# Key norms around the start of attention: an earlier scaling, a root by Newton steps, and work moved between attention's first blocks

## The chip, the cores and the metric

One core of a Trainium2 chip. The metric is the device time of one execution in microseconds; three executions of the kernel before gave 1094.52, 1094.96 and 1095.26 us, median 1094.96.

## The reference, cut to what matters

One decoder block of 512 tokens, width 1024. The part around the change is the attention with eight heads: queries and keys are normalised by head, rotated and scored in 128-query blocks.

```python
kv = (rms_norm(kv_lat, g_kva) @ w_kvb).reshape(B, S, H, QK_NOPE + V_DIM)
k_nope = rms_norm(kv[..., :QK_NOPE], g_k_nope)
v = kv[..., QK_NOPE:]
...
def block(args):
    q_i, i = args
    s = jnp.einsum('bhqd,bhkd->bhqk', q_i, kh).astype(jnp.float32)
    ...
    prob = jax.nn.softmax(s, axis=-1).astype(vh.dtype)
    return jnp.einsum('bhqk,bhkd->bhqd', prob, vh)
```

`rms_norm` multiplies by the reciprocal root of the mean square. For the keys this is one number for each token and head.

## The kernel before, in words

Each engine runs a queue of its own, written out by hand; semaphores order them. The stage ahead of attention takes eight steps `s`: steps 0 to 3 project two query heads each, steps 4 to 7 two key heads with their values. In a step TensorE multiplies four token tiles in three passes (high and low parts of fp32), ScalarE writes each tile out of PSUM with its squares and takes a root, and VectorE sums the squares (128 rows x 8 numbers: four tiles by two heads), forms the mean (`mean`, L1409), takes ScalarE's root back as a reciprocal and scales the keys with it (L1774; for the last step `last_k_norm`, L1779 to L1782). `link` makes VectorE wait for an instruction of its own before the next one reads its result. Then TensorE transposes the two heads (`head_T`, by L2141), which waits for the semaphore `qk_n`, and for the PSUM bank, which VectorE frees as it evacuates the heads before (`k_evac`, L1743). `rope_low` (L1730) makes the low parts of one head's rotated query rows, in two halves.

Attention has 32 blocks (8 heads by 4 query blocks; within a head in the order 1, 4, 2, 3 key tiles wide, the last head 1, 2, 3, 4). In the loop's pass `s` TensorE makes the scores of block `s` (L2328 to L2333), transposes the probabilities of block `s` - 1 (L2343) and multiplies those of block `s` - 2 with the values (L2352). The first block of a head waits for that head's rope rows (semaphore `rope_lo`). VectorE takes the maximum of block `s` (L1805), then the reciprocal sum and the scaling of block `s` - 2 (L1811, L1814). ScalarE takes the exponential (L1163) and copies the transposed probabilities. GpSimd adds each scaled block to the other branch (L795) and, between two such additions, splits the output weights: a high part (L804) after even blocks, a low part (L807) after odd ones.

The last two key heads are used from block 24 on. Their transposes stand in TensorE's loop at `s` = 5. SyncE's loads for the stage after attention wait until all 32 blocks are added.

Of the kernel before, what the change touches and what calls it, by code (L numbers as in the profile page):

```python
# [6 lines left out]
def hybrid_block_kernel(nc, a, out):  # L7
# [24 lines left out]
    I32, U32 = mybir.dt.int32, mybir.dt.uint32  # L32
# [45 lines left out]
    with ctx:  # L78
# [827 lines left out]
        def _(act):  # L906
# [194 lines left out]
            for s in range(9):  # L1101
                if s == 6:
                    rope_high(0)
                    rope_high(1)
                if s < 8:
                    for t in range(NT):
                        n = P_Q + 4 * s + t
                        act.wait_ge(pj_done, n + 1)
                        if t == 0:
                            if s >= 1:  # L1110
                                act.wait_ge(qk_ms, s)
                            if 2 <= s < 6:
                                act.wait_ge(tr_done, T_Q + 3 * (s - 2) + 2)
                                act.wait_ge(q_rot, s - 1)
                            elif s >= 6:
                                act.wait_ge(tr_done, step_T(s - 2))
                            if s == 0:
                                act.wait_ge(ln_v, NT)
                        b_ = bank[n % 4]
                        if s < 4:  # L1120
                            src = b_[:, 0:2 * QK].rearrange("p (h d) -> p h d", h=2)
                            act.activation(qc[s % 2][:, t], src, ACT.Copy)
                            act.activation(sqc[:, t], src, ACT.Square).then_inc(pj_free[n % 4], 1)
                        else:
                            src = b_[:, :].rearrange("p (h d) -> p h d", h=2)
                            c = s - 4
                            act.activation(qc[s % 2][:, t, :, 0:NOPE], src[:, :, 0:NOPE], ACT.Copy)
                            act.activation(sqc[:, t, :, 0:NOPE], src[:, :, 0:NOPE], ACT.Square)
                            act.activation(V[:, t, 2 * c:2 * c + 2, :], src[:, :, NOPE:], ACT.Copy).then_inc(pj_free[n % 4], 1)
                        if t == (0 if s == 6 else 1) and s + 1 < 8:  # L1130
                            qkv_split(s + 1)
                if s == 7:
                    T = T_K + 4
                    act.wait_ge(tr_done, T + 1)
                    act.activation(kT[:, 4, :], bank[4 + T % 2][:, :], ACT.Copy).then_inc(tr_free[T % 2], 1)
                if 1 <= s <= 4:
                    c = s - 1
                    for h in range(2):
                        T = T_Q + 3 * c + h
                        act.wait_ge(tr_done, T + 1)  # L1140
                        act.activation(qT[:, 2 * c + h, :], bank[4 + T % 2][:, :], ACT.Copy, scale=gqk).then_inc(tr_free[T % 2], 1)
                if s < 8:
                    act.wait_ge(qk_ms, s + 1)
                    n = 16 if s < 4 else 8
                    act.activation(ssq[:, 0:n], msq[:, 0:n], ACT.Sqrt).then_inc(qk_rt, 1)
# [254 lines left out]
        def _(dve):  # L1400
            steps = [0]

            def link(ins):
                steps[0] += 1
                ins.then_inc(dve_step, 1)
                dve.wait_ge(dve_step, steps[0])
# [318 lines left out]
            def rope_low(h, halves=(0, 1)):  # L1725
                r0, r1 = ROPE * (h % 2), ROPE * (1 - h % 2)
                dve.wait_ge(rope_hi, h + 1)
                for half in halves:
                    cols = slice(half * SEQ // 2, (half + 1) * SEQ // 2)
                    dve.tensor_tensor(q_st[r1:r1 + ROPE, h % 2, cols], qrT[r0:r0 + ROPE, h // 2, cols],  # L1730
                                      q_st[r0:r0 + ROPE, h % 2, cols].bitcast(F32), ALU.subtract).then_inc(rope_lo, 1)
# [2 lines left out]
                gate_a(g)  # L1734

            def k_evac(c, b0):
                if c == 1:
                    rope_low(0)
                    rope_low(1)
                for h in range(1 if c == 2 else 0, 2):  # L1740
                    T = T_K + 2 * c + h
                    dve.wait_ge(tr_done, T + 1)
                    dve.tensor_copy(kT[:, 2 * c + h, :], bank[b0 + T % 2][:, :]).then_inc(tr_free[T % 2], 1)  # L1743

            for s in range(8):
                if 2 <= s <= 5:
                    T = T_Q + 3 * (s - 2) + 2
                    dve.wait_ge(tr_done, T + 1)
                    dve.tensor_copy(qrT[:, s - 2, :], bank[4 + T % 2][:, :]).then_inc(tr_free[T % 2], 1)
                if s + 1 < 8:  # L1750
                    qkv_split(s + 1)
                if s < 8:
                    sq = sqc.rearrange("p t h d -> p (t h) d")
                    if s == 7:
                        dve.wait_ge(pj_free[1], (P_Q + 4 * s) // 4 + 1)
                        link(dve.tensor_reduce(ssq[:, 0:4], sq[:, 0:4, 0:NOPE], AX.X, ALU.add))
                    dve.wait_ge(pj_free[3], (P_Q + 4 * s) // 4 + 1)
                    if s < 4:
                        link(dve.tensor_reduce(ssq[:, 8:16], sq[:, :, NOPE:QK], AX.X, ALU.add))
                    r0 = 4 if s == 7 else 0  # L1760
                    link(dve.tensor_reduce(ssq[:, r0:8], sq[:, r0:8, 0:NOPE], AX.X, ALU.add))
                    if s < 4:
                        mean(msq[:, 8:16], ssq[:, 8:16], ROPE, EPS)
                    mean(msq[:, 0:8], ssq[:, 0:8], NOPE, EPS).then_inc(qk_ms, 1)
                if 5 <= s < 7:
                    k_evac(s - 5, 4)
                if s < 7:
                    dve.wait_ge(qk_rt, s + 1)
                    n = 16 if s < 4 else 8
                    link(dve.reciprocal(msq[:, 0:n], ssq[:, 0:n]))  # L1770
                    z = qc[s % 2].rearrange("p t h d -> p (t h) d")
                    if s < 4:
                        dve.tensor_tensor(z[:, :, NOPE:QK], z[:, :, NOPE:QK], rep(msq[:, 8:16], [P, 8, ROPE], 2), ALU.mult)
                    dve.tensor_tensor(z[:, :, 0:NOPE], z[:, :, 0:NOPE], rep(msq[:, 0:8], [P, 8, NOPE], 2),  # L1774
                                      ALU.mult).then_inc(qk_n, 1)

            def last_k_norm():
                dve.wait_ge(qk_rt, 8)
                link(dve.reciprocal(msq[:, 0:8], ssq[:, 0:8]))  # L1779
                z = qc[1].rearrange("p t h d -> p (t h) d")  # L1780
                dve.tensor_tensor(z[:, :, 0:NOPE], z[:, :, 0:NOPE], rep(msq[:, 0:8], [P, 8, NOPE], 2),
                                  ALU.mult).then_inc(qk_n, 1)  # L1782
# [10 lines left out]
            for s in range(NA + 2):  # L1793
                if s == NA + 1:
                    mT_low(0)
                if s == 1:
                    k_evac(2, 4)
                if s == 2:
                    last_k_norm()
                if s == 7:  # L1800
                    k_evac(3, 6)
                if s < NA:
                    W = (head_block(s)[1] + 1) * P
                    dve.wait_ge(s_done, s + 1)
                    dve.tensor_reduce(nm[:, s % 4:s % 4 + 1], bank[s % 2][:, 0:W], AX.X, ALU.max,  # L1805
                                      negate=True).then_inc(nm_ready, 1)
                if s >= 2:
                    n = s - 2
                    h, i = head_block(n)
                    dve.wait_ge(pv_done, n + 1)  # L1810
                    link(dve.reciprocal(rinv[:, n % 4:n % 4 + 1], rs[:, n % 4:n % 4 + 1]))  # L1811
                    if n >= 2:
                        dve.wait_ge(ya_add, n - 1)
                    dve.scalar_tensor_tensor(otmp[n % 2], bank[2 + n % 2][:, 0:VD], rinv[:, n % 4:n % 4 + 1],  # L1814
                                             sigb[:, i, h * VD:(h + 1) * VD], ALU.mult, ALU.mult).then_inc(o_ready, 1)
                if s % NT < 2 and 2 <= s // NT + 1 < H:
                    rope_low(s // NT + 1, (s % NT,))
# [317 lines left out]
        def _(pe):  # L2135
# [176 lines left out]
            for i in range(4):  # L2312
                pe.wait_ge(pj_free[i], P_WO // 4)
            for s in range(NA + 2):
                if s == 5:
                    head_T(7, b0=6)
                if s == 2 * H:
                    for i in range(2):
# [323 lines left out]
```

## Time and profile before

| | |
|---|---|
| median of three executions | 1094.96 us |
| the profiled execution, its own time | 1094.87 us |
| its span in the profile | 1093.1 us |
| TensorE's, VectorE's, ScalarE's, GpSimd's busy share | 98%, 85%, 74%, 38% |
| TensorE's granted clock, in all 40 slices | 9 (90% of full speed or more) |
| the eight projection steps end at | about 272 us |
| attention | about 273 to 337 us |

The span is the time from the first to the last instruction; the execution's own time is 1.8 us longer. A busy share is an average over the whole program: VectorE's 85% comes mostly from the experts' stage behind attention, and says nothing of the few microseconds at attention's start, for which the timelines of single engines are read.

### The profile page before, as it was taken

What the parts mean: (1) busy time and instruction counts of PE and PEld (TensorE: products, weight loads), DVE (VectorE), ACT (ScalarE), POOL (GpSimd) and SP (SyncE); (2) the same over time, 40 slices, a digit from 0 to 9 for tenths busy, and PEclk for the clock granted to TensorE, in tenths of its full rate; (3) what the DMA queues carried; (4) which work ended last, traced back from release to release, by engine and by line L of the source; (5) the groups of instructions that cost most, each with busy time, mean ns of one, the idle gap of its engine ahead of it and who ended that gap; (6) DMA issues with size and microseconds to landing.
All of it is one profiled execution on the core that took longest, in us unless ns stands there. A gap on an engine that the chain in (4) does not pass through costs nothing.

```text
span 1093.1 us, 17847 instructions
## 1 busy us (share of the span) xinstructions
PE 1076.3 (98%) x5416; PEld 901.6 (82%) x5416; DVE 933.8 (85%) x1313; ACT 803.9 (74%) x1287; POOL 414.3 (38%) x482
## 2 busy tenths in 40 slices
PE   7999999999999999999999999999999999999998
PEld 6988888797788888888888888888888888888787
DVE  5998879577764578999999999999999999999865
ACT  7854545377553345988888888888998898888671
POOL 1100003052573003455555555555555555454300
PEclk9999999999999999999999999999999999999999
DMA  8765435023204099999999999999999999999632
GB/s 300 219 159 146 124 106 185 22 69 131 76 2 154 39 362 349 382 367 386 393 395 384 394 391 388 390 393 393 396 397 397 395 397 393 390 392 357 182 146 77
DMA packets 76504, 301.12 MB, mean 275 GB/s; under 512 B 15459, under 2 KB 20870, under 8 KB 51494
## 3 DMA queue, kind: packets, MB, share of 16 engines
q1 hardware_dynamic: 54400, 258.33, 59.3%
q0 software_dynamic: 21408, 40.04, 15.4%
q10 hardware_dynamic: 646, 2.12, 0.5%
q8 instruction: 28, 0.46, 0.2%
q14 instruction: 22, 0.18, 0.0%
HBM read 294.05 MB, written 42.07 MB: 307 GB/s over the span
## 4 chain that ended last, share of the span: by engine, by line
PE 93%; DVE 3%; ACT 2%; POOL 1%; issue 1%; DMA 0%; ACTq 0%; POOLq 0%; DVEq 0%
PE bank L2516 11%; PE bank L2518 11%; PE bank L2517 11%; PE bank L2150 7%; PE bank L2544 5%; PE bank L2543 5%; PE bank L2542 5%; PE bank L2481 5%; PE bank L2244 3%; PE bank L2243 3%; PE bank L2242 3%; PE bank L2186 2%; PE bank L2187 2%; PE bank L2190 2%; PE bank L2141 2%; PE bank L2395 1%
## 5 line engine op out<-in xcount | busy, mean ns | idle before, releaser
L2022 DVE TENSOR_TENSOR arena_r<-arena,win_r 128x1024 fp32r<-128x1024 f32 x252 | 291.8, 1219 | 22.1 <-ACT win_r L1296 20.1
L1296 ACT ACTIVATE win_r<-arena 128x1024 fp32r<-128x1024 f32 x252 | 246.5, 1069 | 0.5 <-DMA resid<-in_w_exp_up 0.5
L2516 PE MATMUL bank<-win_r,work_r 128*128 128x512 f32 x512 | 206.5, 403 | 0.6 <-issue 0.6
L2517 PE MATMUL bank<-win_r,x_low_r 128*128 128x512 f32 x512 | 199.5, 390 | 0.0
L2518 PE MATMUL bank<-arena_r,work_r 128*128 128x512 f32 x504 | 197.4, 392 | 0.0
L2002 DVE TENSOR_TENSOR arena_r<-arena,hT_r 128x1024 fp32r<-128x1024 f32 x128 | 150.3, 1214 | 0.5 <-ACT hT_r L1304 0.5
L872 POOL DMA_INDIRECT moe_sum<-ya,sidx x64 | 104.0, 1626 | 109.9 <-ACT ya L1332 104.5
L2518 PEld LDWEIGHTS bank<-arena_r,work_r 128*128 128x128 f32 x504 | 94.6, 188 | 21.7
L2516 PEld LDWEIGHTS bank<-win_r,work_r 128*128 128x128 f32 x512 | 96.7, 189 | 18.8 <-issue 0.7
L2517 PEld LDWEIGHTS bank<-win_r,x_low_r 128*128 128x128 f32 x512 | 96.4, 188 | 18.6
L847 POOL COPY small<-ya 128x1 f32 (+1 forms) x64 | 109.8, 1716 | 1.5 <-DMA ya<-h_rows,gidx 1.5
L2542 PE MATMUL bank<-hT_r,work_r 128*128 128x512 f32 x256 | 105.2, 411 | 0.0
L2544 PE MATMUL bank<-arena_r,work_r 128*128 128x512 f32 x256 | 100.5, 393 | 0.0
L2543 PE MATMUL bank<-hT_r,work_r 128*128 128x512 f32 x256 | 100.0, 391 | 0.0
L832 POOL DMA_INDIRECT ya<-h_rows,gidx x66 | 69.9, 1060 | 52.9 <-POOL gidx L829 52.9
L1987 DVE TENSOR_TENSOR x_low_r<-bank,work_r 128x512 fp32r<-128x512 f32 x128 | 81.9, 680 | 0.3 <-ACT work_r L1269 0.3
L1269 ACT ACTIVATE work_r<-bank 128x512 fp32r<-128x512 f32 x128 | 69.5, 595 | 13.4 <-PE bank L2481 11.5
L1329 ACT ACTIVATE ya<-bank 128x512 f32<-128x512 f32 x64 | 38.4, 600 | 48.5 <-PE bank L2544 48.5
L2150 PE MATMUL bank<-win_r,arena_r 128*128 128x512 f32 (+1 forms) x224 | 72.6, 373 | 0.3 <-DVE win_r L1701 0.3
L1304 ACT ACTIVATE hT_r<-arena 128x1024 fp32r<-128x1024 f32 x65 | 68.9, 1062 | 0.0
L829 POOL COPY gidx<-slot_tokens 128x1 uint32 (+1 forms) x66 | 15.1, 229 | 140.9 <-PE bank L2481 132.0
L1312 ACT ACTIVATE hT_r<-arena 128x1024 fp32r<-128x1024 f32 x63 | 67.0, 1063 | 0.0
(406 smaller groups left out, 2423.5 us busy)
## 6 DMA issues: line engine op xcount, KB each, us to landing
arena<-in_w_exp_down SPq DMA_DIRECT2D x64, 1024.0 KB, 12.2
arena<-in_w_exp_gate SPq DMA_DIRECT2D x63, 1024.0 KB, 8.7
arena<-in_w_exp_up SPq DMA_DIRECT2D x63, 1024.0 KB, 12.4
win<-in_w_in SPq DMA_DIRECT2D x10, 1024.0 KB, 5.4
resid<-in_x SPq DMA_DIRECT2D x8, 512.0 KB, 5.8
win<-in_w_in SPq DMA_DIRECT2D x2, 2048.0 KB, 9.3
win<-in_w_o SPq DMA_DIRECT2D x2, 2048.0 KB, 7.7
arena<-in_w_ple_gate SPq DMA_DIRECT2D x2, 2048.0 KB, 13.8
```

The source lines that it names most:

```text
L847: pool.tensor_copy(wt[j % 4], rows_[:, D + j:D + j + 1] if q is None else rows_[:, bass.ds(q * RING + (D + j), 1)]).then_inc(wt_ready, 1)
L872: pool.indirect_dma_start(sums[j % 2], bass.IndirectOffsetOnAxis(sidx[j % 2][0:NS, 0:1], 0), yo[j % 2][0:NS], None, bounds_check=last_toke ...
L1296: act.activation(gu_hi[n % 2][:, :, cols], raw[:, :, cols], ACT.Copy).then_inc(gu_hi_r, 1)
L2002: dve.tensor_tensor(wdn_lo[j % RING][:, k, :], wdn[j % RING][:, k, :], wdn_hi[j % 2][:, k, :].bitcast(F32), ALU.subtract).then_inc(dn_lo, 1)
L2022: dve.tensor_tensor(low_[:, :, cols], raw[:, :, cols], gu_hi[n % 2][:, :, cols].bitcast(F32), ALU.subtract).then_inc(gu_lo_r, 1)
L2150: last = pe.matmul(bank[b_][:, 0:width], l, r, start=(i == 0), stop=(i == len(pairs) - 1))
L2516: pe.matmul(b_, x_hi[:, k, :], w_hi, start=(k == 0), stop=False)
L2517: pe.matmul(b_, x_lo[:, k, :], w_hi, start=False, stop=False)
L2518: last = pe.matmul(b_, x_hi[:, k, :], low_[:, :, k * FF:(k + 1) * FF], start=False, stop=(k == KD - 1))
L2542: pe.matmul(b_, hi, w_hi, start=(k == 0), stop=False)
L2543: pe.matmul(b_, lo, w_hi, start=False, stop=False)
L2544: last = pe.matmul(b_, hi, wdn_lo[n % RING][:, k, cols], start=False, stop=(k == KF - 1))
```

## The change

For the next to last key heads (step 6) VectorE scales the keys as soon as ScalarE has their root; the evacuation of the heads before and the rope rows come after it. The rope rows of head 0 stand behind the first half of the last step's sum of squares, those of head 1 in attention's pass 2. The last key heads' mean is finished in pass 1, and their reciprocal root is not taken by ScalarE and a reciprocal, but by VectorE alone: a first guess from the number's bits and three Newton steps, spread over passes 3, 4 and 5, each behind the maximum of its block; the scaling follows in pass 5. The transposes of the last heads move from pass 5 to pass 7, their evacuation from ahead of the maximum of block 7 to ahead of that of block 9; the evacuation of head 5 moves from pass 1 to pass 0.

```diff
@@ ScalarE, after each step
-                if s < 8:
+                if s < 7:
                     act.wait_ge(qk_ms, s + 1)
@@ VectorE, k_evac
-                if c == 1:
-                    rope_low(0)
-                    rope_low(1)
@@ VectorE, steps
                     if s == 7:
                         dve.wait_ge(pj_free[1], (P_Q + 4 * s) // 4 + 1)
                         link(dve.tensor_reduce(ssq[:, 0:4], sq[:, 0:4, 0:NOPE], AX.X, ALU.add))
+                        rope_low(0)
+                        continue
...
-                if 5 <= s < 7:
-                    k_evac(s - 5, 4)
+                if s == 5:
+                    k_evac(0, 4)
                 if s < 7:
                     dve.wait_ge(qk_rt, s + 1)
...
+                if s == 6:
+                    k_evac(1, 4)
+
+            def last_k_mean():
+                dve.wait_ge(pj_free[3], (P_Q + 4 * 7) // 4 + 1)
+                link(dve.tensor_reduce(ssq[:, 4:8], sqc.rearrange("p t h d -> p (t h) d")[:, 4:8, 0:NOPE], AX.X, ALU.add))
+                mean(msq[:, 0:8], ssq[:, 0:8], NOPE, EPS).then_inc(qk_ms, 1)
+
+            def last_k_root(step):
+
+                m, y, w = msq[:, 0:8], ssq[:, 0:8], ssq[:, 8:16]
+                if step == 0:
+                    dve.wait_ge(qk_ms, 8)
+                    link(dve.tensor_scalar(y.bitcast(I32), m.bitcast(I32), 1, None, ALU.arith_shift_right))
+                    link(dve.tensor_scalar(y.bitcast(I32), y.bitcast(I32), -1.0, 1597463007.0, ALU.mult, ALU.add))
+                link(dve.tensor_tensor(w, y, y, ALU.mult))
+                link(dve.tensor_tensor(w, w, m, ALU.mult))
+                link(dve.tensor_scalar(w, w, -0.5, 1.5, ALU.mult, ALU.add))
+                link(dve.tensor_tensor(m if step == 2 else y, y, w, ALU.mult))
 
             def last_k_norm():
-                dve.wait_ge(qk_rt, 8)
-                link(dve.reciprocal(msq[:, 0:8], ssq[:, 0:8]))
@@ VectorE, attention
-                if s == 1:
-                    k_evac(2, 4)
-                if s == 2:
-                    last_k_norm()
-                if s == 7:
+                if s == 9:
                     k_evac(3, 6)
                 if s < NA:
...
                                       negate=True).then_inc(nm_ready, 1)
+                if s == 0:
+                    k_evac(2, 4)
+                if s == 1:
+                    last_k_mean()
+                if s == 2:
+                    rope_low(1)
+                if 3 <= s <= 5:
+                    last_k_root(s - 3)
+                if s == 5:
+                    last_k_norm()
@@ TensorE, attention
-                if s == 5:
+                if s == 7:
                     head_T(7, b0=6)
```

VectorE's queue from the mean of the next to last key heads to the maximum of block 0, before (L1730 rope rows, L1743 evacuation, L1774 scaling of the keys, L1756 and L1761 sums of squares, L1805 maximum):

```order
L1409 TENSOR_SCALAR small<-small 128x8 [waits dve_step]
L1730 TENSOR_TENSOR rope_q_r<-arena,rope_q_r 64x256 [waits rope_hi_ready]
L1730 TENSOR_TENSOR rope_q_r<-arena,rope_q_r 64x256
L1730 TENSOR_TENSOR rope_q_r<-arena,rope_q_r 64x256 [waits rope_hi_ready]
L1730 TENSOR_TENSOR rope_q_r<-arena,rope_q_r 64x256
L1743 COPY arena<-bank 128x512 [waits tr_done] x2
L1770 RECIPROCAL small<-small 128x8 [waits qk_rt]
L1774 TENSOR_TENSOR arena<-arena,small 128x8x128 [waits dve_step]
L1756 TENSOR_REDUCE small<-arena 128x4 [waits pj_free1]
L1761 TENSOR_REDUCE small<-arena 128x4 [waits pj_free3,dve_step]
L1409 TENSOR_SCALAR small<-small 128x8 [waits dve_step]
L1805 TENSOR_REDUCE small<-bank 128x1 [waits s_done]
```

and now (L1772 scaling, L1740 evacuation, L1753 sum, L1816 maximum):

```order
L1409 TENSOR_SCALAR small<-small 128x8 [waits dve_step]
L1768 RECIPROCAL small<-small 128x8 [waits qk_rt]
L1772 TENSOR_TENSOR arena<-arena,small 128x8x128 [waits dve_step]
L1740 COPY arena<-bank 128x512 [waits tr_done] x2
L1753 TENSOR_REDUCE small<-arena 128x4 [waits pj_free1]
L1730 TENSOR_TENSOR rope_q_r<-arena,rope_q_r 64x256 [waits rope_hi_ready,dve_step]
L1730 TENSOR_TENSOR rope_q_r<-arena,rope_q_r 64x256
L1816 TENSOR_REDUCE small<-bank 128x1 [waits s_done]
```

The scaling, for which TensorE's transposes wait, has moved from behind four rope rows and two evacuations to right behind the reciprocal.

VectorE's queue from the maximum of block 4 to that of block 6, before (L1811 reciprocal sum, L1814 scaling of a block):

```order
L1805 TENSOR_REDUCE small<-bank 128x1 [waits s_done]
L1811 RECIPROCAL small<-small 128x1 [waits pv_done]
L1814 SCALAR_TENSOR_TENSOR arena<-bank,small,arena 128x128 [waits ya_add,dve_step]
L1730 TENSOR_TENSOR rope_q_r<-arena,rope_q_r 64x256 [waits rope_hi_ready]
L1805 TENSOR_REDUCE small<-bank 128x1 [waits s_done]
L1811 RECIPROCAL small<-small 128x1 [waits pv_done]
L1814 SCALAR_TENSOR_TENSOR arena<-bank,small,arena 128x128 [waits ya_add,dve_step]
L1730 TENSOR_TENSOR rope_q_r<-arena,rope_q_r 64x256 [waits rope_hi_ready]
L1805 TENSOR_REDUCE small<-bank 128x1 [waits s_done]
```

and now, from the maximum of block 5 to that of block 6 (L1789 to L1792 a Newton step, L1796 the scaling of the last key heads, L1832 and L1835 a block's reciprocal sum and scaling):

```order
L1816 TENSOR_REDUCE small<-bank 128x1 [waits s_done]
L1789 TENSOR_TENSOR small<-small 128x8
L1790 TENSOR_TENSOR small<-small 128x8 [waits dve_step]
L1791 TENSOR_SCALAR small<-small 128x8 [waits dve_step]
L1792 TENSOR_TENSOR small<-small 128x8 [waits dve_step]
L1796 TENSOR_TENSOR arena<-arena,small 128x8x128 [waits dve_step]
L1832 RECIPROCAL small<-small 128x1 [waits pv_done]
L1835 SCALAR_TENSOR_TENSOR arena<-bank,small,arena 128x128 [waits ya_add,dve_step]
L1730 TENSOR_TENSOR rope_q_r<-arena,rope_q_r 64x256 [waits rope_hi_ready]
L1816 TENSOR_REDUCE small<-bank 128x1 [waits s_done]
```

Five instructions have come between the two maxima; four of the same kind stand behind the maximum of block 4, six behind that of block 3.

## Rows read from the trace of the kernel before

**Rows 1.** The profile's chain that ended last, shares of the span by engine.

```profile
PE 93%; DVE 3%; ACT 2%; POOL 1%; issue 1%; DMA 0%; ACTq 0%; POOLq 0%; DVEq 0%
```

**Rows 2.** The chain in order of time, 262 to 300 us: start us, us, what.

```profile
268.62 0.75 DVE rope_q_r L1730 x2
...
270.16 1.20 DVE arena L1743 x2
...
271.63 1.11 DVE arena L1774
272.77 0.69 DVE small L1756
...
281.89 0.87 PE bank L2141 x8
```

**Rows 3.** Timeline, TensorE: start us, us, engine line op tiles [idle before <-releaser].

```profile
271.32 0.39 PE L2150 MATMUL bank<-win_r,arena_r 128*128 128x512 f32 x1
...
272.91 1.09 PE L2141 MATMUL bank<-ident,arena 128*128 128x128 f32 x8 [1.20 <-DVE arena L1774]
...
273.98 0.30 PE L2331 MATMUL bank<-arena_r,rope_q_r 128*128 128x128 f32 x1
```

**Rows 4.** Timeline, ScalarE.

```profile
268.62 0.21 ACT L1145 ACTIVATE small<-small 128x8 f32<-128x8 f32 x1 [1.49 <-DVE small L1409]
...
274.63 1.28 ACT L1163 ACT_TABLE_LOAD   x1
...
275.92 0.37 ACT L1163 ACTIVATE arena<-bank,small 128x128 f32<-128x128 f32 x1
```

**Rows 5.** Timeline, VectorE: the maxima of blocks 1, 3, 4, 5, 6, 9 and 13.

```profile
275.95 0.69 DVE L1805 TENSOR_REDUCE small<-bank 128x1 f32<-128x512 f32 x1 [0.56 <-PE bank L2333]
...
279.50 0.56 DVE L1805 TENSOR_REDUCE small<-bank 128x1 f32<-128x384 f32 x1 [0.52 <-PE bank L2333]
...
281.15 0.29 DVE L1805 TENSOR_REDUCE small<-bank 128x1 f32<-128x128 f32 x1
...
284.19 0.69 DVE L1805 TENSOR_REDUCE small<-bank 128x1 f32<-128x512 f32 x1 [0.91 <-PE bank L2333]
...
286.00 0.42 DVE L1805 TENSOR_REDUCE small<-bank 128x1 f32<-128x256 f32 x1
...
292.06 0.69 DVE L1805 TENSOR_REDUCE small<-bank 128x1 f32<-128x512 f32 x1 [0.40 <-PE bank L2333]
...
299.37 0.69 DVE L1805 TENSOR_REDUCE small<-bank 128x1 f32<-128x512 f32 x1
```

**Rows 6.** VectorE's groups of instructions, 274 to 337 us: busy us, mean ns | idle.

```profile
L1814 DVE SCALAR_TENSOR_TENSOR arena<-bank,small,arena 128x128 f32<-128x128 f32 x32 | 11.2, 351 | 1.1
...
L1811 DVE RECIPROCAL small<-small 128x1 f32<-128x1 f32 x32 | 5.2, 163 | 11.9 <-PE bank L2352 11.2
```

**Rows 7.** Instructions of line L1730: ns min/median/max, first and last start us.

```profile
L1730 DVE TENSOR_TENSOR rope_q_r<-arena,rope_q_r x16: 410/420/770, 268.6 to 322.6; 64x256 fp32r<-64x256 f32 x16
```

**Rows 8.** Timelines of GpSimd and VectorE, around 253.8, 261.0 and 282 us.

```profile
253.71 0.74 POOL L767 TENSOR_TENSOR work<-arena 128x256 f32<-128x256 f32 x1
253.83 0.65 DVE L1409 TENSOR_SCALAR small<-small 128x8 f32<-128x8 f32 x1
...
261.02 0.17 DVE L1409 TENSOR_SCALAR small<-small 128x8 f32<-128x8 f32 x1
...
281.31 0.46 POOL L795 TENSOR_TENSOR ya<-ya,arena 128x128 f32<-128x128 f32 x1 [1.15 <-DVE arena L1814]
281.73 1.27 POOL L807 TENSOR_TENSOR win_r<-win,arena_r 128x512 fp32r<-128x512 f32 x1
...
282.51 0.77 DVE L1730 TENSOR_TENSOR rope_q_r<-arena,rope_q_r 64x256 fp32r<-64x256 f32 x1
```

**Rows 9.** Timeline, VectorE in the router: two linked small operations, one behind the other.

```profile
401.74 0.18 DVE L1901 TENSOR_SCALAR work<-work 128x32 f32<-128x32 f32 x1
401.95 0.18 DVE L1902 TENSOR_SCALAR work<-work 128x32 f32<-128x32 f32 x1
```

More of the change, by code:

```diff
@@ L1759, in _ @@
                         link(dve.tensor_reduce(ssq[:, 8:16], sq[:, :, NOPE:QK], AX.X, ALU.add))
-                    r0 = 4 if s == 7 else 0
-                    link(dve.tensor_reduce(ssq[:, r0:8], sq[:, r0:8, 0:NOPE], AX.X, ALU.add))
+                    link(dve.tensor_reduce(ssq[:, 0:8], sq[:, 0:8, 0:NOPE], AX.X, ALU.add))
                     if s < 4:
```

## The prediction

> **What bounds the kernel now.** I read the page first: 93% of the chain that ended last is TensorE's [rows 1]. So the change can count only where TensorE waits, and every such wait that it touches lies between the end of the last key projection (about 271.5 us) and the first heads of attention (about 300 us). There I followed the chain in order of time [rows 2], then TensorE's, ScalarE's and VectorE's timelines [rows 3 to 5]. Two things are to be seen. First, TensorE's last projection matmul starts at 271.32, but its next transposes start at 272.91 [rows 3], behind a VectorE queue of two pairs of rope rows, two evacuations and only then the normalising product of the next to last key heads [rows 2]. Second, in attention each block goes round TensorE, VectorE's maximum and ScalarE's exponential. Heads settle at 7.31 us (a head's 512-wide block has its maximum at 292.06, the next at 299.37), but the one before took 7.87 (284.19 to 292.06) [rows 5]: VectorE's extra work shows there at once. "Block n" below is the n-th score block, from 0; four make a head.
>
> **The sum.** All against the profiled execution, 1094.87 us (0.09 under the median of 1094.96, which changes nothing).
>
> *Step A, the start of attention.* The mean of the next to last key heads is followed by ScalarE's root at 268.62, 0.21 long [rows 4]. Now the reciprocal comes straight behind it (0.21, by the pace of linked small operations, 401.74 to 401.95 [rows 9]) and the normalising product (1.11 [rows 2]): done at 270.2 instead of 272.7. TensorE is then not held at all, and transposes right behind its projection, at 271.55: 1.36 earlier. What is late next is VectorE's queue behind the product: two evacuations 1.20, the first half of the squares' sum 0.69 and one pair of rope rows 0.75 [rows 2] end near 272.9. TensorE's first matmul on rope rows, at 273.98 before [rows 3], can start near 273.0. So blocks 0 to 3 come 0.95 earlier, block 1's maximum at 275.0 for 275.95 [rows 5]. The table load before the first exponential stays; only the square root in front of it goes. It took 1.28, with the exponential 1.29 after its start [rows 4]; started 1.36 earlier it ends near 274.6, ahead of block 1's maximum, and costs nothing.
>
> The Trainium skill's ScalarE: Activation LUTs page (What ACT_TABLE_LOAD costs) gives some 2.66 us for every switch of table set, a drain included. By that the first exponential would not come before 275.9, block 1's would wait for it, the lead would be some 0.4 and not 0.95, and the sum 0.55 worse; the rows here show no such drain, and I go by them.
>
> *Step B, to block 4.* After block 1's maximum (0.69) VectorE has the second half of the squares (0.69), their mean (0.2), block 2's maximum (0.42), the second pair of rope rows (0.75) and block 0's reciprocal and scaling (0.16 and 0.35 [rows 6]): 3.26, to 278.3. Block 3's scores are there at 279.50 less 0.95, 278.55, so all this hides in VectorE's waits. From here it has none. Block 3's maximum 0.56 [rows 5], six Newton operations at 0.21, 1.26, and block 1's scaling 0.51 put block 4's maximum at 280.88 for 281.15: the lead is down to 0.27.
>
> *Step C, to block 5.* Block 4's maximum 0.29, four Newton operations 0.84, scaling 0.51, half a rope pair 0.42 [rows 7]: 2.06, so block 5's maximum could be at 282.94 instead of 284.19, a lead of 1.25. Part of that is the last heads' transposes, 0.87 on the chain just ahead of block 5 [rows 2], which now stand ahead of block 7. But GpSimd is at work here. When VectorE has scaled block 1, GpSimd adds it (281.31, 0.46) and at once makes a low part of the output weights (281.73, 1.27) [rows 8]. A rope row issued beside that took 0.77 and ended 0.28 after it, against a median of 0.42 [rows 7, 8]; and a 128x8 scalar operation, the very size of Newton's, took 0.65 and ended within 0.03 us of a GpSimd product (253.71, 0.74), against 0.17 [rows 8]. The second Newton pass now stands 0.3 us behind that scaling: its first product meets the add, its second the 1.27 product. The price is between 0 (held by nothing) and 1.47 (the whole product and the rest of the add); I take 1.35, as both rows speak for being held to the end. Block 5 at 284.29: 0.10 late.
>
> The Trainium skill's SBUF — State Buffer page (Who interferes with whom) says that a VectorE instruction with two SBUF inputs and a GpSimd instruction that reads SBUF exclude each other, the later one blocked for the earlier one's whole length. It says nothing of a least size, and no row shows a small two-input product beside GpSimd; by the rule the term is the 1.35, without it 0 and the sum 1.1.
>
> *Step D, to block 6.* Block 5's maximum 0.69, the last Newton pass 0.84, the normalising product of the last key heads 1.11, scaling 0.51, half a rope pair 0.42: 3.57, in the place of 1.81 (284.19 to 286.00 [rows 5]). VectorE waits for nothing in it. For GpSimd's next operation I add 0.2, between 0 and an add's 0.46. Block 6's maximum comes at 288.06 instead of 286.00: 2.06 late.
>
> *Step E, to block 9.* Two evacuations of the last key heads (1.20) move from ahead of block 7 to ahead of block 9, a 512-wide one. Before, they cost 7.87 less 7.31, 0.56. In the new place they cost between nothing and all of it, so -0.56 to +0.64 more; I take +0.4, since VectorE comes late to this place and GpSimd's work with it. The last heads' transposes, 0.87, stand where TensorE now waits for block 6's late maximum: 0, at most 0.87.
>
> Removed besides: ScalarE's last root, 0.21, off the path. No DMA moves; SyncE's next loads wait for attention's last block, so a shift here goes through to the end one for one. Sum: 2.06 + 0.4 = **+2.45 us, 1097.3 us**.
>
> **The rivals.**
> 1. *The small operations slip past GpSimd.* Nothing is held in steps C and D: block 6 at 286.51, 0.51 late, with step E 0.9: 1095.8. For it: they are short, and may fall between GpSimd's operations. Against: the 128x8 row [rows 8].
> 2. *Faster: VectorE never decides block 6.* The head start of step A stays and the transposes' 0.87 is gained too, if the passes and the last product fit into waits. Price: -0.95 - 0.87, 1093.1. It decides from the point where block 5's maximum plus 3.57 ends before 286.00, block 5 at 282.4 or earlier. By step C the best is 282.94, so Newton's operations would have to be clearly shorter than 0.21.
> 3. *Worse: held at every pass.* Step C 1.47, D 0.46, E +0.64 and the transposes' 0.87 unhidden: 3.95, 1098.8. For it: every late VectorE step delays GpSimd's and so lays them on top of each other again.
> 4. *The change doesn't do what it says*, if a table switch costs more than its row or the transposes are not freed at 271.55: the start's 0.95 goes, and block 6 would then be late by up to 3, near 1098.
>
> **How the numbers follow.** Forecast 0.57, rival 1 0.20, rival 2 0.10, rival 3 0.10, rival 4 0.03. From the bounds, the lowest end of steps C to E is about -0.05, the highest 3.95. I leave rival 2 and the top of rival 3 out: 1095.0 to 1098.6; the forecast's own range is 1096.5 to 1098.2. About 0.2%, 2.2 us, is what a measurement of this kernel tells from no change; the forecast lies just past it. Slower by more: some six in ten of the forecast, rival 3 and most of rival 4, 0.47. Within it: the rest of the forecast, rival 1 and most of rival 2, 0.49. Faster by more: 0.04.
>
> **What would show it.** Right: transposes at 271.55 without a wait; first exponential near 274.6; block 4's maximum near 280.9; a Newton product of the second pass lasting over a microsecond beside a GpSimd product; VectorE without idle time from block 3's to block 6's maximum, the latter near 288; the shift constant from block 12 on. Wrong: Newton operations all at 0.17 to 0.21 (rival 1), block 6's maximum before 286 (rival 2), or block 1's maximum not earlier (rival 4). A shift after 337 us that attention doesn't have would break the whole argument.

## The result and the profile after

| | before | after |
|---|---|---|
| median of ten executions | 1094.91 us | 1097.80 us |
| lowest to highest | 1094.35 to 1096.74 | 1096.25 to 1099.86 |
| the profiled execution, its own time | 1094.87 us | 1096.25 us |
| its span | 1093.1 us | 1094.5 us |

The ratio of the medians is 1.0028, its 95% interval 1.0020 to 1.0037: the change costs 2.9 us (2.2 to 4.1). The profiled execution is the shortest of the ten; what the longer ones have besides is found in the experiments.

In the trace of after the whole program reaches the end of the projection steps 0.52 us earlier, which the change has nothing to do with. The mark is the sum of squares of step 6, which stands ahead of everything that was changed. VectorE's timeline, before:

```profile
267.16 1.22 DVE L1761 TENSOR_REDUCE small<-arena 128x8 f32<-128x1024 f32 x1 [1.25 <-ACT hT L1129]
```

and after:

```profile
266.64 1.22 DVE L1759 TENSOR_REDUCE small<-arena 128x8 f32<-128x1024 f32 x1 [1.25 <-ACT hT L1129]
```

All shifts below are counted from this mark, so 0.52 is added to a time of after (in other traces, what their mark says) before it is held against one of before.

TensorE's timeline of after answers to [rows 3]; the last three rows have no counterpart before:

```profile
270.80 0.39 PE L2171 MATMUL bank<-win_r,arena_r 128*128 128x512 f32 x1
271.03 1.03 PE L2162 MATMUL bank<-ident,arena 128*128 128x128 f32 x8
...
272.52 0.30 PE L2352 MATMUL bank<-arena_r,rope_q_r 128*128 128x128 f32 x1
...
285.31 0.66 PE L2364 MATMUL bank<-ident,arena 128*128 128x128 f32 x4 [2.02 <-ACT arena L1163]
...
286.54 1.09 PE L2162 MATMUL bank<-ident,arena 128*128 128x128 f32 x8 [0.34 <-DVE arena L1796]
287.47 0.81 PE L2349 MATMUL bank<-arena 128*128 128x384 f32 x2
```

The transposes now follow the last projection matmul with nothing between them, where [rows 3] had 1.20 us of waiting. But a new wait of 2.02 us stands ahead of the transposes of block 5's probabilities (and one of 1.12 ahead of block 9's). Before, the row of block 5's carries no wait:

```profile
285.75 0.66 PE L2343 MATMUL bank<-ident,arena 128*128 128x128 f32 x4
```

ScalarE, as in [rows 4]:

```profile
272.67 1.28 ACT L1163 ACT_TABLE_LOAD   x1
273.96 0.37 ACT L1163 ACTIVATE arena<-bank,small 128x128 f32<-128x128 f32 x1
```

VectorE from block 1's maximum (L1816; L1805 in [rows 5]) to block 13's, with the Newton operations (L1787 to L1792), the scaling of the last key heads (L1796), and the rope row (L1730) and evacuations (L1740) ahead of block 9's:

```profile
274.50 0.69 DVE L1816 TENSOR_REDUCE small<-bank 128x1 f32<-128x512 f32 x1 [0.56 <-PE bank L2354]
...
278.04 0.56 DVE L1816 TENSOR_REDUCE small<-bank 128x1 f32<-128x384 f32 x1 [0.35 <-PE bank L2354]
278.51 0.38 DVE L1787 TENSOR_SCALAR small<-small 128x8 int32<-128x8 int32 x1
...
279.13 0.17 DVE L1789 TENSOR_TENSOR small<-small 128x8 f32<-128x8 f32 x1
279.33 0.17 DVE L1790 TENSOR_TENSOR small<-small 128x8 f32<-128x8 f32 x1
...
280.41 0.28 DVE L1816 TENSOR_REDUCE small<-bank 128x1 f32<-128x128 f32 x1
280.61 0.45 DVE L1789 TENSOR_TENSOR small<-small 128x8 f32<-128x8 f32 x1
281.09 1.20 DVE L1790 TENSOR_TENSOR small<-small 128x8 f32<-128x8 f32 x1
282.32 0.17 DVE L1791 TENSOR_SCALAR small<-small 128x8 f32<-128x8 f32 x1
...
283.76 0.69 DVE L1816 TENSOR_REDUCE small<-bank 128x1 f32<-128x512 f32 x1
284.37 0.25 DVE L1789 TENSOR_TENSOR small<-small 128x8 f32<-128x8 f32 x1
...
285.26 1.23 DVE L1796 TENSOR_TENSOR arena<-arena,small 128x1024 f32<-128x1024 f32 x1
...
287.42 0.42 DVE L1816 TENSOR_REDUCE small<-bank 128x1 f32<-128x256 f32 x1
...
292.01 0.77 DVE L1730 TENSOR_TENSOR rope_q_r<-arena,rope_q_r 64x256 fp32r<-64x256 f32 x1
292.70 1.27 DVE L1740 COPY arena<-bank 128x512 f32<-128x512 f32 x2
293.90 0.67 DVE L1816 TENSOR_REDUCE small<-bank 128x1 f32<-128x512 f32 x1
...
301.18 0.69 DVE L1816 TENSOR_REDUCE small<-bank 128x1 f32<-128x512 f32 x1
```

GpSimd beside it:

```profile
278.25 0.62 POOL L804 CAST arena_r<-win 128x512 fp32r<-128x512 f32 x1
280.57 0.46 POOL L795 TENSOR_TENSOR ya<-ya,arena 128x128 f32<-128x128 f32 x1 [1.71 <-DVE arena L1835]
280.99 1.28 POOL L807 TENSOR_TENSOR win_r<-win,arena_r 128x512 fp32r<-128x512 f32 x1
...
283.99 0.60 POOL L804 CAST arena_r<-win 128x512 fp32r<-128x512 f32 x1
...
291.22 1.27 POOL L807 TENSOR_TENSOR win_r<-win,arena_r 128x512 fp32r<-128x512 f32 x1
```

Behind block 3's maximum (278.04), up to and with block 6's (287.42), no VectorE row carries a wait. The product of the second Newton pass, 128x8 as its sisters of 0.17 us, lasted 1.20, to 281.09 + 1.20 = 282.29; GpSimd's product beside it ended at 280.99 + 1.28 = 282.27. The row ahead of it lasted 0.45, to 281.06, and GpSimd's addition ended at 281.03.

### The profile page after: what moved, and what is told of

Its sections match the earlier page's. It is cut to its first block, busy times and chain, and to the rows that moved or that the text cites. A ratio compares the mean times of both kernels' runs of the same rounds, so it can differ in the third digit from the quotient of the medians.

```text
span 1094.5 us, 17861 instructions
## 1 busy us (share of the span) xinstructions
PE 1075.6 (98%) x5416; PEld 900.9 (82%) x5416; DVE 937.5 (86%) x1326; ACT 803.7 (73%) x1286; POOL 413.9 (38%) x482
## 4 chain that ended last, share of the span: by engine, by line
PE 94%; DVE 3%; ACT 1%; POOL 1%; issue 1%; DMA 0%; ACTq 0%; DVEq 0%
PE bank L2537 11%; PE bank L2539 11%; PE bank L2538 11%; PE bank L2171 8%; PE bank L2565 5%; PE bank L2564 5%; PE bank L2563 5%; PE bank L2502 5%; PE bank L2265 3%; PE bank L2264 3%; PE bank L2263 3%; PE bank L2207 2%; PE bank L2211 2%; PE bank L2208 2%; PE bank L2162 2%; PE bank L2416 1%
```

## The experiments

The question was twofold. Does VectorE's queue make the shift in attention, and with which of its parts? And why is the median 1.55 us above the profiled execution? The theory for the first is steps B to E of the prediction; the rivals are that holding costs nothing, or that the moved scaling and evacuation make the loss. For the second the theory came from the list of executions. The granted clock is the share of its full speed that TensorE gets, 1.00 at the higher of its two levels (2.4 GHz) and 0.50 at the lower (1.2 GHz); its mean is taken over an execution. Seven of the ten have a mean granted clock of 0.998, the other three 0.999 or 1.0, and those three are the three shortest.

How late a block's maximum is against before, in us, counted from the mark:

| kernel | block 1 | 4 | 5 | 6 | 9 | 13 | 31 |
|---|---|---|---|---|---|---|---|
| the change (first trace) | -0.93 | -0.22 | 0.09 | 1.94 | 2.36 | 2.33 | 2.35 |
| the change, trace at clock 0.998 | -0.91 | -0.20 | 0.12 | 1.98 | 3.60 | 3.58 | 3.59 |
| split withheld | -0.93 | -0.43 | -1.30 | 0.46 | 1.57 | 1.55 | 1.56 |
| no Newton operations | -0.93 | -1.00 | -1.86 | -0.83 | -0.41 | -0.44 | -0.42 |
| early scaling alone | -0.93 | -0.76 | -0.75 | -0.75 | -0.74 | -0.76 | -0.76 |
| fourth Newton step | -0.90 | -0.18 | 0.14 | 2.80 | 5.40 | 5.39 | 5.39 |
| evacuation at block 12 | -0.89 | -0.18 | 0.13 | 1.99 | 1.33 | 1.57 | 1.66 |
| all late, no Newton | -0.92 | -0.77 | -1.63 | -1.63 | -1.60 | -1.38 | -1.29 |
| wait filled | -0.94 | -0.22 | 0.09 | 1.95 | 2.37 | 2.35 | 2.34 |

**The change again.** No edit.

> The changed kernel once more, for a trace beside the others. If VectorE's queue between block 3's and block 6's maximum is all there is to it, the time is some 2.0 to 2.9 us over the kernel before, the second Newton pass again has a product that lasts over a microsecond beside GpSimd's, and block 13's maximum stands 1.8 to 2.4 us later than before. If the part of the median that the first trace of the change does not show (it had +1.4 us) comes from TensorE's granted clock, a trace with a mean clock of 0.998 shows stretches below 1.0 that the first has not, and the time lost in them is 1 to 3 us.

1098.79 us (1097.12 to 1099.21), before 1094.58 beside it; ratio 1.0037 (1.0023 to 1.0050). That is 4.2 us over it, where 2.0 to 2.9 were expected of VectorE's queue alone. Its trace, again of an execution at clock 1.0, repeats the first to 0.02 us in every block. Three of its five executions are at 0.998, and they are the three longest; what happens in them this trace can't show.

**The output weights' split withheld.** GpSimd, behind its addition of block n (the lines below use `m` where they had `n`):

```diff
-    (c, k), low_part = divmod(n // 2, KD), n % 2
+    for m in () if n < 4 else (2 * n - 8, 2 * n - 7) if n < 8 else (n,):
+        (c, k), low_part = divmod(m // 2, KD), m % 2
```

> The change, with GpSimd's split of the output weights (high and low parts) withheld behind blocks 0 to 3 and done twice as fast behind blocks 4 to 7, so that no split stands beside Newton's second pass. Theory (VectorE is the bound there, and the split holds its small operations): blocks 4 to 5 are 2.1 us apart and not 3.35, block 6's maximum is only 0.4 to 0.9 us later than before, and the time is 1.2 to 1.7 us under that of the changed kernel, some 1.0 to 1.5 us over the kernel before. Rival (the hold costs nothing on the path, the number of linked operations alone does): the long product is gone from the trace, and the time is that of the changed kernel within 0.3 us.

1096.16 us (1095.73 to 1098.15), ratio 1.0017 (1.0008 to 1.0026): 2.6 us under the changed kernel run beside it. Blocks 4 and 5 are 2.17 us apart, as the theory has it, and block 6 is late by 0.46. The rival falls: beside Newton's operations the split costs 1.39 at block 5 (0.09 less -1.30), of which 0.21 stands at block 4 already (-0.22 less -0.43), where the cast is gone from beside the first Newton operation. VectorE, in the second pass and then ahead of block 9 (lines of this kernel stand one number higher, L1791 for the second product):

```profile
280.75 0.15 DVE L1790 TENSOR_TENSOR small<-small 128x8 f32<-128x8 f32 x1
280.94 0.32 DVE L1791 TENSOR_TENSOR small<-small 128x8 f32<-128x8 f32 x1
...
290.89 1.45 DVE L1731 TENSOR_TENSOR rope_q_r<-arena,rope_q_r 64x256 fp32r<-64x256 f32 x1
```

and GpSimd:

```profile
280.77 0.45 POOL L795 TENSOR_TENSOR ya<-ya,arena 128x128 f32<-128x128 f32 x1 [2.11 <-DVE arena L1836]
...
290.77 1.28 POOL L808 TENSOR_TENSOR win_r<-win,arena_r 128x512 fp32r<-128x512 f32 x1
```

The product is down to 0.32 (the addition holds it still). But the split, made up at twice the pace, now meets a rope row: 1.45 us for 0.42, with the last heads' evacuation behind it. So the shift grows by 1.1 at block 9 (0.46 to 1.57), where the changed kernel's grew by 0.42; attention keeps 0.8, less than the 1.2 to 1.7 expected. The medians show more than that: all eleven executions are at clock 1.0, three of the changed kernel's five beside them are not.

**No Newton operations.**

```diff
+                dve.wait_ge(qk_ms, 8)
...
-                if 3 <= s <= 5:
-                    last_k_root(s - 3)
```

> The change without its fourteen Newton operations: the last two key heads are scaled by their mean square in place of its reciprocal root, all else stands where the change put it. Theory (Newton's operations with their hold make up nearly all of the loss): 14 x 0.21 plus a hold of some 1.2 us fall out of VectorE's queue, part of which the waits take that then open: 2.4 to 2.8 us under the changed kernel, which is the time of the kernel before or up to 0.5 us less; block 5's maximum some 1.9 us and block 6's 0.7 us earlier than before. Rival (the moved scaling of the last heads and their moved evacuation make the loss): still 1 us or more over the kernel before, with block 9's maximum late by as much.

1093.98 us (1093.63 to 1095.70), ratio 0.9998 (0.9989 to 1.0007): 0.6 under before in the medians, within the interval nothing; 4.8 under the changed kernel, more than the 2.4 to 2.8 expected. In the trace attention is 0.42 earlier than before, 2.77 less than with Newton (2.35 + 0.42), as the theory has it. The other 2 us of the medians is what the traces at clock 1.0 don't show. The rival falls.

**The early scaling alone.** In the kernel before, `k_evac(1, 4)` goes behind the scaling of step 6, `rope_low(0)` behind the first half of step 7's sum, `rope_low(1)` behind block 2's maximum; all else stays.

> The kernel before with the early part of the change alone: keys of the next to last heads scaled ahead of evacuations and rope rows, the first pair of rope rows behind the first half of the last sum of squares, the second behind the maximum of block 2; the last root stays with ScalarE, the last heads' scaling, transposes and evacuation where they were. Theory (step A holds): the transposes follow the last projection matmul without a wait, blocks 0 to 3 come 0.9 us earlier and all 32 blocks keep it: 0.7 to 1.0 us under the kernel before. Rival (a later VectorE step takes the head start back, the second pair of rope rows or the last heads' scaling in pass 2): 0.3 us or less.

1093.85 us (1093.15 to 1094.38), ratio 0.9993 (0.9984 to 1.0002): 0.7 under before, which the times alone don't separate. The trace does: 0.93 earlier at block 1, and 0.74 to 0.76 from block 4 to block 31.

**A fourth Newton step.**

```diff
-                link(dve.tensor_tensor(m if step == 2 else y, y, w, ALU.mult))
+                link(dve.tensor_tensor(m if step == 3 else y, y, w, ALU.mult))
...
                 if s == 5:
+                    last_k_root(3)
```

> The change with a fourth Newton step behind the third in pass 5: four more linked 128x8 operations on VectorE where it waits for nothing. Theory: each costs its 0.21 us, so block 6's maximum, 1.94 later than before in the changed kernel (both counted from the last step's sum of squares), is 2.78 later, block 13's 3.2 instead of 2.33; the median is 0.8 to 1.2 us over the changed kernel's. Rival (VectorE is not the bound at block 6, the late scores are): block 6's maximum does not move and the time stays within 0.2 us. If the lower granted clock of many executions comes from TensorE's long wait ahead of block 6, no fewer of this kernel's executions have a mean clock of 0.998 than of the changed kernel's.

1099.57 us (1097.42 to 1100.27), ratio 1.0039 (1.0025 to 1.0053). Block 6 is late by 2.80, 0.86 more than in the changed kernel, for four operations at 0.21: VectorE is the bound there. Block 13, though, is late by 5.39 and not 3.2, and the median is 1.8 over the changed kernel's 1097.80 where 0.8 to 1.2 was expected. Here the profiled execution is one at clock 0.997 (four of five are). TensorE's timeline, with a transposing group and a score matmul that took 1.09 and 0.81 in the changed kernel above:

```profile
285.79 0.70 PE L2365 MATMUL bank<-ident,arena 128*128 128x128 f32 x4 [2.03 <-ACT arena L1163]
...
287.82 1.97 PE L2163 MATMUL bank<-ident,arena 128*128 128x128 f32 x8 [0.89 <-DVE arena L1796]
289.58 1.49 PE L2350 MATMUL bank<-arena 128*128 128x384 f32 x2
```

In the windows of this trace the granted clock is 0.64 from 286 to 287, 0.50 from 287 to 293, 0.95 from 293 to 294 and 1.00 after that: the lower of TensorE's two levels, 1.2 GHz, from about 286.3, half a microsecond behind the end of the wait of 2.03 us. The wait of 0.89 lies in the lowered stretch already.

**The evacuation of the last heads at block 12.**

```diff
-                if s == 9:
+                if s == 12:
                     k_evac(3, 6)
```

> The change with the evacuation of the last key heads ahead of the maximum of block 12, 128 wide, and not of block 9, 512 wide. Theory (step E: late at block 9, the two evacuations delay its maximum): block 9's maximum comes 0.5 to 1.2 us earlier than in the changed kernel, and of that 0.4 to 1.0 us is left at block 13, since ahead of the narrow block the evacuations lie mostly in VectorE's wait; the time is 0.4 to 1.0 us under the changed kernel. Rival (the evacuation costs the same wherever it stands): block 9 earlier, block 13 as in the changed kernel, no gain.

1097.12 us (1095.55 to 1098.67), ratio 1.0020 (1.0011 to 1.0029): 0.7 under the changed kernel's 1097.80. Its eight executions at 0.998 have a median of 1097.5 (the changed kernel's seventeen, counted below, 1098.4), the three at 1.0 have 1095.9 (1096.4), so the gain shows at either clock. Block 9 comes 1.03 earlier, and 0.69 of that is left at block 31. VectorE's timeline, with the two evacuations and the maximum of block 12:

```profile
298.43 1.28 DVE L1740 COPY arena<-bank 128x512 f32<-128x512 f32 x2
299.63 0.28 DVE L1816 TENSOR_REDUCE small<-bank 128x1 f32<-128x128 f32 x1
```

Block 12's maximum waits for them (late by 2.53, block 11's by 1.34), but at block 13 only 1.57 is left of that. TensorE's wait ahead of block 5's probabilities, 2.02, is untouched by this edit.

**All of it late, without Newton.** The kernel with the early scaling alone, and:

```diff
-                if s == 2:
+                if s == 7:
                     last_k_norm()
-                if s == 7:
+                if s == 12:
                     k_evac(3, 6)
-                if s == 5:
+                if s == 10:
                     head_T(7, b0=6)
```

(the scaling now behind the pass's maximum, not ahead of it).

> The kernel before with the early scaling, and with the last key heads' scaling moved out of pass 2 to pass 7, their transposes to pass 10 and their evacuation ahead of block 12; their root stays with ScalarE. No Newton operation. Theory (the loss is Newton's operations alone; the places that the change chose after the wide blocks are better than those of before if VectorE is not late there): the early scaling's 0.75 us stays, the transposes' 0.87 leave the path ahead of block 5, and part of it is paid at pass 10: 1.0 to 1.6 us under the kernel before. Rival (each moved piece costs as much at its new place as at its old one): 0.6 to 0.9 us under the kernel before, as with the early scaling alone.

1093.12 us (1092.64 to 1094.12), ratio 0.9985 (0.9976 to 0.9994): 1.6 us under the kernel before, clear of the interval, and 4.7 under the changed one. Ahead of block 5 the transposes' 0.87 is gone from the path (-0.77 at block 4, -1.63 at block 5); behind block 12, 1.3 of the 1.6 is left, 0.5 more than the early scaling alone has (0.76). TensorE's row of those transposes carries no wait and stands between two blocks' work:

```profile
289.93 0.83 PE L2354 MATMUL bank<-hT,x_low 128*128 128x128 f32 x6
290.60 1.04 PE L2143 MATMUL bank<-ident,arena 128*128 128x128 f32 x8
```

All eleven executions are at clock 1.0.

**The changed kernel a third time.**

> The changed kernel a third time, for its trace alone. If VectorE's queue sets the shift, block 13's maximum stands 2.3 us later than before, counted from the last step's sum of squares, for the third time. If its mean clock is 0.998, the stretch with the lower clock is in the trace: theory, right behind TensorE's longest wait in attention, between block 5's and block 6's maximum; rival, at the program's end, where the last output leaves.

1096.38 us, one execution, clock 1.0; block 13 late by 2.34. It had nothing to show of the clock.

**TensorE's wait filled.**

```diff
+                if s == 6:
+                    for _ in range(24):
+                        pe.matmul(bank[7][:, 0:P], identb[:, :], negmask[:, :], start=True, stop=True)
                 if 1 <= s <= NA:
```

> The changed kernel with 24 small matmuls (128x128, bf16, about 0.07 us each) in TensorE's queue behind the scores of block 6, where it waited 2.0 us for the exponential of block 5; nobody reads what they write. VectorE's queue stays as the change left it. Theory (TensorE's long wait there brings its clock down to the lower level in most executions, as in the trace with the fourth Newton step, on top of the 2.3 us that VectorE costs): block 13's maximum stays 2.3 to 2.4 later than before, the mean clock is 0.999 or 1.0 in all or nearly all executions, and the median is 1.0 to 1.8 us under the changed kernel's, 1.8 to 2.6 us over the kernel before. Rival (the lower clock comes by itself, or has nothing to do with this wait): as many executions at 0.998 as without the matmuls, and the median of the changed kernel within 0.4 us.

1096.76 us (1096.66 to 1097.50), ratio 1.0020 (1.0011 to 1.0029). TensorE's timeline:

```profile
283.64 1.50 PE L2357 MATMUL bank<-negmask,identb 128*128 128x128 bf16 x24
285.83 0.66 PE L2367 MATMUL bank<-ident,arena 128*128 128x128 f32 x4 [0.68 <-ACT arena L1163]
```

VectorE's shift is the same to 0.02 us, but no execution of the eleven is at 0.998, and from the shortest to the longest it is 0.84 us.

**The changed kernel beside it.**

> The changed kernel beside the kernel with its wait filled, on the same chip. Theory: most executions with a mean clock of 0.998 or 0.997, the others some 1.5 to 2 us shorter; median 2.5 to 4.3 us over the kernel before. Rival (the share of lowered executions depends on the chip or on what ran before, not on the kernel): the same share as in the kernel with the wait filled.

1097.82 us (1095.92 to 1099.29), the same chip as the filled one: 1.06 over it, and 3.4 us from the shortest to the longest. Seven of eleven executions are at 0.998, and each is longer than every one of the filled kernel. The other four, at 1.0, took 1095.9 to 1096.7, and the filled kernel's 1096.7 to 1097.5: where the clock stays up, the filling gains nothing. The profiled execution is one of the seven. Its windows (us and, of each engine, busy us and number of instructions; then TensorE's granted clock):

```profile
core 0: us, PE busy (x) PEld busy (x) DVE busy (x) ACT busy (x) POOL busy (x), PEclk, DMA share, GB/s
284.00:286.00 2.00, 0.41 (x4) 0.23 (x2) 1.83 (x7) 0.39 (x1) 1.24 (x2) 1.00 0.00 0
286.00:288.00 2.00, 1.22 (x8) 1.03 (x9) 1.90 (x5) 0.55 (x3) 0.00 (x0) 0.85 0.00 0
288.00:290.00 2.00, 2.00 (x9) 1.76 (x8) 1.33 (x5) 0.99 (x3) 1.85 (x2) 0.50 0.00 0
290.00:292.00 2.00, 2.00 (x13) 1.48 (x12) 0.56 (x1) 0.09 (x2) 1.03 (x3) 0.79 0.00 0
292.00:294.00 2.00, 2.00 (x19) 1.76 (x18) 0.94 (x5) 1.95 (x7) 0.87 (x2) 1.00 0.00 0
```

and TensorE's timeline there:

```profile
286.44 0.66 PE L2364 MATMUL bank<-ident,arena 128*128 128x128 f32 x4 [2.03 <-ACT arena L1163]
...
287.66 1.97 PE L2162 MATMUL bank<-ident,arena 128*128 128x128 f32 x8 [0.34 <-DVE arena L1796]
289.42 1.49 PE L2349 MATMUL bank<-arena 128*128 128x384 f32 x2
290.14 0.97 PE L2352 MATMUL bank<-arena_r,rope_q_r 128*128 128x384 f32 x1
```

Up to block 6 this trace is the first one (1.98 for 1.94). Then TensorE, which waited 2.03 us, runs the last heads' transposes and block 7's scores at the lower level, and block 13 is late by 3.58 and not 2.33: 1.25 us more. With the wait filled this happens in none of eleven executions, without that in seven; so it is the wait that the change made that lets the clock fall, though not every time. The rival, that the lowered executions belong to the chip, falls.

The Trainium skill's TensorE: Matmul & The Clock Gate page (HAM oscillation — how this bites in real kernels) describes this form: TensorE waits between two pieces of work (there for a transfer, and longer, every time), its clock falls, and the next piece runs at the lower level. The rows agree in form, with 0.50 behind a wait of 2.03 us; here the wait is for ScalarE, and four of these eleven executions keep the clock.

## Why the prediction was right, and where not

It said 1097.3 us; the median is 1097.8, in the range 1095.0 to 1098.6. The loss of 2.9 is past the 2.2 that a measurement tells from no change, for which the prediction had a chance of 0.47 beside 0.49 for no change. Step by step, times of after moved by the 0.52:

| step | predicted | measured |
|---|---|---|
| A, last heads but one transposed | 271.55 | 271.55 |
| A, first rope matmul | 273.0 | 273.04 |
| A, block 1's maximum | 275.0 | 275.02 |
| A, table load ends | 274.6 | 274.47 |
| B, block 4's maximum | 280.88 | 280.93 |
| C, block 5's maximum | 284.29 | 284.28 |
| C, the hold in the second pass | 1.35 | 1.31 |
| D, block 6's maximum | 288.06 | 287.94 |
| E, more at block 9 | 0.4 | 0.42 |
| sum in attention | 2.45 | 2.35 |

The terms of the sum as printed, 2.06 and 0.4, make 2.46; the 1097.3 is the same.

**Step A** holds, and the kernel with the early scaling alone shows it by itself; its 0.93 shrinks to 0.75 there. The table load cost nothing: the exponential starts 1.29 after it, as in [rows 4], at once when the load ends. By the 2.66 us of the Trainium skill's ScalarE: Activation LUTs page (What ACT_TABLE_LOAD costs), which the prediction weighed, it would by estimate have come some 1.4 us later; the trace does not agree, with the exponential at the load's end.

**Step B** holds, with one cost it did not have: the first Newton operation lasted 0.38, to 278.89, and GpSimd's cast ended at 278.87. Block 4 was late by only 0.05 against the forecast, because the step's other terms came out 0.17 shorter: 2.37 us from block 3's maximum to block 4's, 0.21 of it the hold, where 2.33 were forecast. To that extent the agreement is luck.

**Step C** was the open term, between 0 and 1.47. The two held rows take 282.32 less 280.61, 1.71 where two free ones take 0.40: 1.31. With the split away, block 5 comes 1.39 earlier, 1.18 of it from this step. The rule of the Trainium skill's SBUF — State Buffer page (Who interferes with whom), that the later of the two is blocked for the earlier one's whole length, holds here for a 128x8 product too, which ended 0.02 behind GpSimd's, and rival 1 (the small operations slip past) falls.

**Step D** took 3.66 from block 5's maximum to block 6's, for 3.77 forecast. The allowance of 0.2 for GpSimd was 0.08: the row of 0.25 for 0.17, which ended at 284.62, beside a cast that ended at 284.59. The fourth Newton step, 0.86 for 0.84, confirms that each operation is paid there.

**Step E** held with 0.42. That it is the place that costs is shown by the evacuation at block 12, which gives 0.69 back. The rope row ahead of it was held too, 0.77 beside GpSimd's 1.27.

**What was missing** is a term, not a size. The prediction asked what TensorE waits for, and let its waits cost their length alone. It did not ask what a wait of 2 us does to TensorE's clock. In 27 executions of the changed kernel 17 are at 0.998, with a median of 1098.4 (1097.6 to 1099.9), and ten at 0.999 or 1.0, with 1096.4 (1095.9 to 1097.2); the 69 executions of before that were timed beside the repeats are all at 0.999 or 1.0. The difference of 2.0 in the medians is the price of the lower clock; one trace shows 1.25 of it in attention. In the trace with the fourth Newton step, whose lowered stretch is twice as long, it is 2.2 (5.39 less 2.35 and 0.86). So the price differs from execution to execution; that this makes up the whole difference is not shown. The forecast of 1097.3 lies between the two groups and belongs to neither. That the shift is the same from block 13 to block 31, and stays so to 1000 us, was as said. Between 1000 and 1042 us the eleven other traces gain 0.3 to 0.8 on the one trace of before, whatever their kernel, so the spans differ by less than attention does: 1.4 for 1.83. The sum was thus 0.5 to 0.9 too high for an execution at full clock (1096.4 less 1094.9 is 1.5, and with the wait filled 1096.76 less 1094.79 is 2.0) and lacked some 2 us for the others. That the forecast is only 0.5 off the median is in part luck: these two errors stand against each other.

Rivals 2 and 3 did not come: block 6 was late by 1.94, and attention by 2.35, not 3.95. What the transposes of the last heads cost at their new place no run shows by itself; it is contained in the 0.42 of step E. Rival 3's number, 1098.8, is near the executions at lower clock, but by another mechanism.

## What to carry to other kernels

A chain of dependent operations on 128x8 numbers is not small where its engine is the bound for a moment: fourteen of them took 2.9 us of VectorE's queue and some 1.6 more beside GpSimd, and 2.8 of it reached the end of attention. Look for work of that kind that can be left on an engine that is idle there, and move instead what has a late deadline behind narrow blocks or into waits (the scaling, transposes and evacuation gained 0.5 us in attention that way, on top of the early scaling's 0.76). And where a change makes a new wait of TensorE of some 2 us, read the granted clock behind it in more than one execution.

## What the runs showed of the hardware that was not expected

- TensorE's clock fell to its lower level (0.50) behind a wait of 2.03 us and stayed there for some 3 us in one trace and 7 in another, though TensorE was busy for most of that stretch; what it ran took 1.97 for 1.09 and 1.49 for 0.81 us. The same wait of 2.02 left the clock at 1.00 in the first trace; which it will be differs from execution to execution. In the kernel with the split withheld, whose trace has a wait of 1.82 us ahead of block 9's probabilities, all eleven executions were at 1.0.
- 24 matmuls that nobody reads, 1.50 us in that wait, made the median 1.06 us shorter, by keeping the clock at 1.00.
- A 128x8 operation with a single input was held not only by a product of GpSimd's, as in [rows 8], but by its cast too: 0.38 for 0.17 us, ending 0.02 behind it.
